# Choosing experts for the dense blocks first, with the low parts on VectorE and three of eight one-hot rows on ScalarE

## The chip, the core and the metric

The kernel runs on one core of a Trainium2 chip. The metric is the device time of one execution in microseconds. Before the change it was 3673.62 (median of three runs, 3673.24 to 3675.31).

## What is computed

One inference step of two layers for 512 prompt tokens and 32 sample tokens, model width 1024. Layer 0 mixes with sliding-window attention and a gated linear recurrence, layer 1 with a convolution module. After each mixer comes the same retrieval from 128 x 128 = 16384 experts of one neuron each, and only this retrieval is touched here:

```python
q = (xb @ w_q).reshape(blk, PEER_HEADS, 2, PEER_DKH)            # 8 heads, two halves
sc = jnp.einsum('nhpd,hpkd->nhpk', q, sub_keys)                 # scores against 128 keys
sv, si = lax.top_k(sc, 16)
cand = sv[:, :, 0, :, None] + sv[:, :, 1, None, :]              # 16 x 16 pairs
cidx = si[:, :, 0, :, None] * 128 + si[:, :, 1, None, :]
fv, fi = lax.top_k(cand, 16)
eidx = jnp.take_along_axis(cidx, fi, axis=-1)
gate = jax.nn.softmax(fv, axis=-1)
act = gelu(jnp.einsum('nd,nhed->nhe', xb, u_tab[eidx]))
y = jnp.einsum('nhe,nhed->nd', gate * act, v_tab[eidx])
```

## The kernel before, in words

Tokens come in five blocks: three dense blocks of 128 prompt tokens (n = 0, 1, 2), and two "lone" blocks, n = 3 (the last 128 prompt tokens) and n = 4 (the 32 samples; 4 x 32 rows, so it has 2 heads per partition in place of 8). The dense blocks compute all 16384 experts with matmuls and weigh them by a gate that is zero for experts not chosen. The lone blocks gather their experts' rows from DRAM one by one and work on VectorE.

Experts go in 128 tiles of 128, each with a unit tile (rows of u) and a value tile (rows of v), 256 tiles a layer. For fp32 accuracy each tile is split in two parts: ScalarE copies it to the high part (`hi`, line 1004, `ring<-raw`), and another engine subtracts this for the low part (`lo`); before the change that is GpSimd for a layer's first 48 tiles (line 1872) and VectorE for the rest (`low`, line 1551). TensorE then does 24 matmuls a unit tile (line 849) or 18 a value tile (line 861). ScalarE applies gelu to a unit's result (line 1075, `ga`). The first 48 tiles (AHEAD) are units; their results are written to DRAM (`units_ahead`) and come back later, since the gates aren't there yet. They pass through four ring slots and four raw buffers, and a unit's result through two PSUM banks: tile i+3's hi copy waits for unit i-1, its matmuls wait for the low part and for the gelu of two units before.

The choice (`select`, lines 1436 to 1523, VectorE) is cut in 15 parts: part 0 forms 50 candidate pairs a head, parts 1 to 4 take the best 16, parts 6 to 14 pick their numbers (`pick`, lines 1487, 1496, 1503). ScalarE takes the Exp of the gate (line 1063), which needs two table loads against gelu. For a dense block TensorE transposes what was chosen (`choice`, line 818), and ScalarE copies it to slT (line 1121): key 1, key 2 and gate of each of 128 rows, along the free dimension.

The gate matrix is made in groups of 8 tokens, 16 groups a block, 48 a layer. For each token VectorE makes two one-hot tiles of 128x128 in `onehots`: key 2 for all eight tokens in one comparison (line 1534), key 1 times the gate with one instruction a token (line 1539). TensorE multiplies them (`gate_group`, line 832), ScalarE copies the result to `stage` (lines 1107, 1113). After 8 groups SyncE writes the 4 MB of `stage` to DRAM (`gate_matrix`, line 433), and the next group's copy waits for this. Buffers for one-hots and for results hold two groups.

Order is written out by hand, a list for each engine, with semaphores between. `FRONT` is how many tiles are stepped through before the first group, `TILES_AFTER[g]` how many after group g; `TILES_BEFORE` is their running sum. The choices before the change stand in the order n = 4, 3, 0 ahead of the first group, then n = 1 and n = 2 beside the groups of blocks 0 and 1. A block's first group needs slT, which needs the whole choice before. After the groups SyncE waits for the gate matrix to be in DRAM, fetches the first gate tile (line 444) and stored unit (line 450), VectorE multiplies them (line 1562), ScalarE and VectorE split the product (lines 1083, 1569), and TensorE starts on value tiles. From there units and values alternate, and VectorE works through gathered rows (lines 1583, 1591) between low parts.

Of the kernel before, what the change touches and what calls it, by code (L numbers as in the profile page):

```python
# [28 lines left out]
P = 128  # L29
# [39 lines left out]
AHEAD, FRONT = 48, 24  # L69
# [36 lines left out]
TILES_AFTER = [0] * (ND // 8)  # L106
for _g in range(ND // 8):
    if _g < 32:
        TILES_AFTER[_g] = {1: 1, 3: 1, 5: 1, 7: 2}.get(_g % 8, 0)
TILES_AFTER[39] = 2  # L110
TILES_BEFORE = [FRONT + sum(TILES_AFTER[:_g]) for _g in range(ND // 8)]
EXP_BEFORE = {3: 0, 8: 1, 19: 2}
# [79 lines left out]
def build(nc, xT, stream, utab, vtab, params, consts, mconsts, reset, keysT, kcacheT, vcache, kvcache_n, state_h, convT,  # L192
          yT, kwin_p, vwin_p, hs_p, cb_p, kwin_s, vwin_s, hs_s, cb_s):
    ctx = ExitStack()
    with ctx:
# [84 lines left out]
        with ExitStack() as z:  # L280
# [27 lines left out]
            slT = sb("slT", [P, 2, 3, P], F32, z)  # L308
# [225 lines left out]
        s_oh = sem("key1_onehots_ready")  # L534
        s_oha = sem("key2_onehots_ready")
# [53 lines left out]
        def _(pe):  # L589
# [220 lines left out]
            def choice(l, n):  # L810

                pe.wait_ge(s_sel, NTILE * l + 3 + n)
# [182 lines left out]
        def _(act):  # L995
# [47 lines left out]

            def retrieval(l):
# [15 lines left out]
            def select_exp(l, i):  # L1060
                H = HEADS[(LONE + DENSE)[i]]
                act.wait_ge(s_gx, NTILE * l + i + 1)
                A.activation(sel[:, 2, 0:H, :], r16[:, 0:H, :], ACT.Exp).then_inc(s_ge, 1)

            def experts(l):
# [53 lines left out]
                for n in DENSE:  # L1119
                    act.wait_ge(s_selT, NDB * l + n + 1)  # L1120
                    A.activation(slT[:, n % 2, :, :], PB[0][:, 0, 0:3 * P].rearrange("p (i r) -> p i r", i=3),
                                 ACT.Copy).then_inc(s_slT, 1)
                    for q in range(16):
                        stage_group(n, q)
                        if q == 6 and n + 1 < NDB:
                            select_exp(l, 3 + n)
# [233 lines left out]
        def _(dve):  # L1360
# [75 lines left out]
            def select(l, i, part):  # L1436

                n = (LONE + DENSE)[i]
# [31 lines left out]
                elif part == 4:  # L1470
                    if done >= 1:
                        dve.wait_ge(s_ge, done)
                    if i >= 3:
                        dve.wait_ge(s_selT, NDB * l + i - 2)
                    elif i == 0 and l:
                        dve.wait_ge(s_selT, NDB * l)
# [48 lines left out]
            def onehots(l, n, q):  # L1525
# [6 lines left out]
                if n * 16 + q >= 2:  # L1532
# [3 lines left out]
                                ALU.is_equal).then_inc(s_oha, 1)  # L1536
                for j in range(8):
# [3 lines left out]
                    if j < 7:  # L1541
                        ch.done(m)
                ch.sync()
                m.then_inc(s_oh, 1)

            def experts(l):
# [57 lines left out]
                for i in range(AHEAD - 3, N_EXP):  # L1604
                    for j in range(ready_by(i - 1), ready_by(i)):
# [461 lines left out]
```

## Time and profile before

| | |
|---|---|
| profiled execution | 3672.08 us, its span 3670.3 us |
| mean granted TensorE clock | 0.947 |
| TensorE matmul busy | 3262.9 us (89%) |
| VectorE busy | 2843.0 us (77%) |
| ScalarE busy | 1284.1 us (35%) |
| GpSimd busy | 1461.5 us (40%) |
| DMA | 807.86 MB, mean 220 GB/s |

Busy shares are means over stages with different limits, so a stage is read by itself: first the busy time of each engine in it, then which wait ends last there. In a row of the timeline a start is followed by a duration; with a count, the duration runs from the first start to the last end. A duration has a short tail that the next instruction of the engine overlaps, so a repeated instruction's price is the distance of two starts. The two layers run the same program in their retrieval.

### The profile page before, as it was taken

The numbers are of one execution on the slowest core, as the hardware profiler recorded it, in microseconds if no ns is written. First come the engines' busy times: TensorE is split into PE (matmuls) and PEld (weight loads), VectorE is DVE, ScalarE is ACT, GpSimd is POOL, SyncE is SP. The second block draws the span as 40 slices with busy tenths as digits, with TensorE's granted clock in tenths as the row PEclk, the third lists the DMA queues.
The fourth block names the chain that finished last, engine by engine and source line by source line (L and its number), as shares of the span: only waits on it lengthen the run. The fifth ranks groups of instructions, "written<-read, shape, count | busy, mean of one in ns | idle before, by whom it ended". The sixth has DMA issues, their size and how long they took to land. (4 is left out here: it accounts for less than half of the span.)

```text
span 3670.3 us, 49481 instructions
## 1 busy us (share of the span) xinstructions
PE 3262.9 (89%) x18573; PEld 2976.5 (81%) x18573; DVE 2843.0 (77%) x5704; ACT 1284.1 (35%) x1735; POOL 1461.5 (40%) x856
## 2 busy tenths in 40 slices
PE   5876899978789999999987879997878999999998
PEld 5876789977778888888877648997767888888887
DVE  4425547999878888888866983799986888888887
ACT  3443222444433333333323222244444333333332
POOL 2210232733135555555542202273213555555553
PEclk9987699989899999999998989998899999999999
DMA  3110121534389999999971142153338999999997
GB/s 116 53 50 1 60 87 61 175 115 165 139 314 371 365 366 362 362 366 363 357 239 58 47 18 79 54 175 124 147 148 291 375 368 361 358 368 364 360 360 260
DMA packets 424991, 807.86 MB, mean 220 GB/s; under 512 B 233953, under 2 KB 259105, under 8 KB 421281
## 3 DMA queue, kind: packets, MB, share of 16 engines
q1 hardware_dynamic: 318960, 454.23, 36.6%
q0 software_dynamic: 94560, 344.45, 25.3%
q10 hardware_dynamic: 11232, 6.01, 1.3%
q8 instruction: 148, 2.42, 0.3%
q14 instruction: 91, 0.74, 0.1%
HBM read 729.52 MB, written 76.08 MB: 219 GB/s over the span
## 5 line engine op out<-in xcount | busy, mean ns | idle before, releaser
L849 PE MATMUL bank<-hh,ring 128*128 128x384 f32 x4096 | 1097.3, 341 | 18.4 <-POOL ring L1872 10.2
L1872 POOL TENSOR_TENSOR ring<-raw,ring 128x1024 fp32r<-128x1024 f32 x182 | 496.9, 2737 | 1110.2 <-ACT ring L1004 1107.3
L861 PE MATMUL bank<-ring,wh 128*128 128x512 f32 x3072 | 831.8, 393 | 22.1 <-DVE wl L1569 22.1
L849 PEld LDWEIGHTS bank<-hh,ring 128*128 128x128 f32 x4096 | 752.8, 191 | 27.9 <-POOL ring L1872 14.6
L1004 ACT ACTIVATE ring<-raw 128x1024 fp32r<-128x1024 f32 x598 | 622.5, 1054 | 241.4 <-PE bank L849 131.1
L849 PE MATMUL bank<-hl,ring 128*128 128x384 f32 x2048 | 692.3, 338 | 0.0
L861 PEld LDWEIGHTS bank<-ring,wh 128*128 128x128 f32 x3072 | 576.5, 188 | 134.5 <-DVE ring L1551 22.7
L1551 DVE TENSOR_TENSOR ring<-raw,ring 128x1024 fp32r<-128x1024 f32 x416 | 508.1, 1222 | 205.7 <-ACT ring L1004 205.5
L1903 POOL DMA_INDIRECT rows<-in_utab,gidx x320 | 450.4, 1408 | 481.8 <-DVE av L1583 378.9
L1903 POOL DMA_INDIRECT rows<-in_vtab,gidx x320 | 490.9, 1534 | 368.6 <-DVE acc L1591 316.1
L610 PE MATMUL bank<-hh,ring 128*128 128x272 f32 x2752 | 494.8, 299 | 78.7 <-DVE hl L1377 43.8
L610 PEld LDWEIGHTS bank<-hh,ring 128*128 128x128 f32 x2752 | 409.8, 196 | 92.7 <-issue 51.5
L861 PE MATMUL bank<-ring,wl 128*128 128x512 f32 x1536 | 474.2, 390 | 0.0
L1075 ACT ACTIVATE ga<-bank 128x384 f32<-128x384 f32 x256 | 124.5, 486 | 990.5 <-PE bank L849 990.3
L1591 DVE SCALAR_TENSOR_TENSOR acc<-rows,wv,acc 128x1024 f32<-128x1024 f32 x316 | 404.3, 1279 | 12.3 <-DVE acc L1591 0.5
L849 PEld LDWEIGHTS bank<-hl,ring 128*128 128x128 f32 x2048 | 390.6, 191 | 6.1
L1583 DVE CUSTOM_DVE_ANT_0 rows<-rows,htok 128x1024 f32<-128x1024 f32 x320 | 381.6, 1218 | 1.0 <-DMA rows<-in_utab,gidx 1.0
L861 PEld LDWEIGHTS bank<-ring,wl 128*128 128x128 f32 x1536 | 289.3, 188 | 64.4
L832 PE MATMUL bank<-oh 128*128 128x128 f32 x1536 | 220.6, 305 | 120.2 <-DVE oh L1539 111.6
L832 PEld LDWEIGHTS bank<-oh 128*128 128x128 f32 x1536 | 207.6, 216 | 132.8 <-DVE oh L1539 123.9
L610 PE MATMUL bank<-hl,ring 128*128 128x272 f32 x1376 | 293.5, 295 | 0.0
L1539 DVE TENSOR_SCALAR oh<-con,slT 128x128 f32<-128x128 f32 x768 | 256.7, 403 | 0.0
(297 smaller groups left out, 3101.5 us busy)
## 6 DMA issues: line engine op xcount, KB each, us to landing
raw<-in_stream SPq DMA_DIRECT2D x342, 512.0 KB, 4.9
raw<-in_vtab SPq DMA_DIRECT2D x256, 512.0 KB, 7.9
gate_matrix<-stage SPq DMA_DIRECT2D x24, 2048.0 KB, 9.3
gt<-gate_matrix SPq DMA_DIRECT2D x256, 192.0 KB, 9.6
units_ahead<-ga SPq DMA_DIRECT2D x96, 192.0 KB, 2.9
gv<-units_ahead SPq DMA_DIRECT2D x96, 192.0 KB, 8.3
rows<-in_utab,gidx POOLq DMA_INDIRECT x320, 8.2
rows<-in_vtab,gidx POOLq DMA_INDIRECT x320, 7.9
```

The source lines that it names most:

```text
L610: m = T.matmul(PA[t % 2][:, a, 0:HALF], w[:, ring_slot(t), k * P:(k + 1) * P], h[:, k, a * HALF:(a + 1) * HALF], start=(k == 0 and i == 0) ...
L832: m = T.matmul(PA[e % 2][:, i // 4, (i % 4) * P:(i % 4 + 1) * P], oh2[:, e % 2, i, :], oh1[:, e % 2, i, :], start=True, stop=True)
L849: m = T.matmul(PB[1][:, (e + 1) % 2, 0:ND], w[:, ring_slot(t), k * P:(k + 1) * P], h[:, k, 0:ND], start=(k == 0 and i == 0), stop=(k == KC ...
L861: m = T.matmul(psum[c][:, a, :], w[:, v_n % WSLOT, c * P:(c + 1) * P], v[:, ring_slot(t), 512 * a:512 * a + 512], start=(v_n == 0 and i == ...
L1004: A.activation(ring_hi[:, ring_slot(t), :], raw[b][:], ACT.Copy).then_inc(s_hi, 1)
L1075: A.activation(ga[:, e % ASLOT, :], PB[1][:, (e + 1) % 2, 0:ND], ACT.Gelu).then_inc(s_ga, 1)
L1539: m = V.tensor_scalar(oh1[:, e % 2, j, :], iota, slT[:, n % 2, 0, c:c + 1], slT[:, n % 2, 2, c:c + 1], ALU.is_equal, ALU.mult)
L1551: V.tensor_tensor(ring_lo[:, ring_slot(t), :], raw[raw_buffer(t)][:], ring_hi[:, ring_slot(t), :].bitcast(F32), ALU.subtract).then_inc(s_l ...
L1583: V.tensor_tensor_reduce(out=rows[:, slot, :], in0=rows[:, slot, :], in1=htok[b][:, :], scale=1.0, scalar=0.0, op0=ALU.mult, op1=ALU.add, ...
L1591: V.scalar_tensor_tensor(out=acc[b][:, :], in0=rows[:, slot, :], scalar=wv[b][:, j:j + 1], in1=acc[b][:, :], op0=ALU.mult, op1=ALU.add).th ...
L1872: nc.gpsimd.tensor_tensor(ring_lo[:, slot, :], raw[buf][:], ring_hi[:, slot, :].bitcast(F32), ALU.subtract).then_inc(s_lo, 1)
L1903: nc.gpsimd.indirect_dma_start(out=rows[:, g % ROW_SLOTS, :], out_offset=None, in_=vtab if is_v else utab, in_offset=bass.IndirectOffsetOn ...
```

## The change

The order of choices becomes 0, 1, 2, then 4, 3 (`SEL_ORDER`). Ahead of the first group VectorE makes only the choice of block 0, in nine quanta with a tile step after each; the lone blocks' choices stand beside the groups of block 2, two parts a group. `FRONT` is 12, and `TILES_AFTER` goes on with its pattern in the third block: 31 tiles inside the groups, so that units 43 to 47 follow the last group. The low parts of tiles 3 to 47 go from GpSimd to VectorE (`ahead` is gone from GpSimd's program). Key 1's rows 0 to 2 of each group (`ACT_OH`) go to ScalarE: Abs(key - iota) and then Relu(gate - gate x distance), which is the gate where the distance is 0, and 0 elsewhere; gates are positive and distances whole. For it slT gets a fourth row, the negated gate.

```diff
-AHEAD, FRONT = 48, 24
+AHEAD, FRONT = 48, 12
...
+TILES_AFTER = [{1: 1, 3: 1, 5: 1, 7: 2}.get(_g % 8, 0) for _g in range(ND // 8)]
+TILES_AFTER[3] = TILES_AFTER[19] = TILES_AFTER[35] = 2
+TILES_AFTER[47] = 0
...
+SEL_ORDER = DENSE + LONE
+SEL_QUANTA = [(0,), (1, 2), (3, 4, 5), (6, 7), (8,), (9, 10), (11,), (12, 13), (14,)]
+EXP_BEFORE = {3: 0}
+ACT_OH = 3
...
+            def onehots(l, n, q):
+
+                e = (ND // 8) * l + n * 16 + q
+                if n * 16 + q >= 2:
+                    act.wait_ge(s_gm, e - 1)
+                if e:
+                    act.wait_ge(s_oha, e)
+                for j in range(ACT_OH):
+                    c = 8 * q + j
+                    ch.done(A.activation(dist[:, j, :], iota, ACT.Abs, scale=-1.0,
+                                         bias=slT[:, n % 2, 0, c:c + 1]))
+                ch.sync()
+                for j in range(ACT_OH):
+                    c = 8 * q + j
+                    m = A.activation(oh1[:, e % 2, j, :], dist[:, j, :], ACT.Relu,
+                                     scale=slT[:, n % 2, 3, c:c + 1], bias=slT[:, n % 2, 2, c:c + 1])
+                m.then_inc(s_oha, 1)
...
                 for n in DENSE:
                     act.wait_ge(s_selT, NDB * l + n + 1)
-                    A.activation(slT[:, n % 2, :, :], PB[0][:, 0, 0:3 * P].rearrange("p (i r) -> p i r", i=3),
-                                 ACT.Copy).then_inc(s_slT, 1)
+                    ch.done(A.activation(slT[:, n % 2, 0:3, :], PB[0][:, 0, 0:3 * P].rearrange("p (i r) -> p i r", i=3),
+                                         ACT.Copy))
+                    ch.sync()
+                    A.activation(slT[:, n % 2, 3, :], PB[0][:, 0, 2 * P:3 * P], ACT.Copy, scale=-1.0)\
+                        .then_inc(s_slT, 1)
+                    act.wait_ge(s_slT, NDB * l + n + 1)
+                    onehots(l, n, 0)
                     for q in range(16):
+                        if q + 1 < 16:
+                            onehots(l, n, q + 1)
                         stage_group(n, q)
...
-                for j in range(8):
+                for j in range(ACT_OH, 8):
...
-                for i in range(3):
-                    for part in range(NPART):
-                        select(l, i, part)
+                dve.wait_ge(s_lo, t0 + 3)
+                for i in range(FRONT):
+                    if i < len(SEL_QUANTA):
+                        for part in SEL_QUANTA[i]:
+                            select(l, 0, part)
+                    tile_step(i)
                 for n in DENSE:
                     for q in range(16):
+                        g = 16 * n + q
                         onehots(l, n, q)
                         if n + 1 < NDB and q >= 1:
-                            select(l, 3 + n, q - 1)
-                dve.wait_ge(s_lo, t0 + AHEAD)
+                            select(l, n + 1, q - 1)
+                        if n + 1 == NDB and q >= 1:
+                            for part in (2 * q - 2, 2 * q - 1):
+                                select(l, NDB + part // NPART, part % NPART)
+                        if g:
+                            for m in range(TILES_AFTER[g - 1]):
+                                tile_step(TILES_BEFORE[g - 1] + m)
```

VectorE, the end of the choice that the first group waits for and the first groups. `pick` and `eidx` belong to the choice, `small` is the signal that it is complete, `ring<-raw,ring` is a low part, `oh` a one-hot tile. Before:

```order
L1509 TENSOR_TENSOR sel<-sel,r 128x128
L1512 TENSOR_SCALAR sel<-eidx 128x128
L1514 TENSOR_SCALAR sel<-sel 128x128
L1516 SCALAR_TENSOR_TENSOR sel<-sel,eidx 128x128
L1523 MEMSET small 128x1
L1534 TENSOR_TENSOR oh<-con,slT 128x1024
L1539 TENSOR_SCALAR oh<-con,slT 128x128 x8
L1534 TENSOR_TENSOR oh<-con,slT 128x1024
L1539 TENSOR_SCALAR oh<-con,slT 128x128 x8
L1445 CAST sif<-si 128x256
```

After, the same place, with the low parts of tiles 11 to 14 between the choice and the first group:

```order
L1536 TENSOR_TENSOR sel<-sel,r 128x128
L1539 TENSOR_SCALAR sel<-eidx 128x128
L1541 TENSOR_SCALAR sel<-sel 128x128
L1543 SCALAR_TENSOR_TENSOR sel<-sel,eidx 128x128
L1550 MEMSET small 128x1
L1575 TENSOR_TENSOR ring<-raw,ring 128x1024 x4
L1561 TENSOR_TENSOR oh<-con,slT 128x1024
L1566 TENSOR_SCALAR oh<-con,slT 128x128 x5
L1561 TENSOR_TENSOR oh<-con,slT 128x1024
L1566 TENSOR_SCALAR oh<-con,slT 128x128 x5
L1474 CAST sif<-si 128x256
```

Five rows a group are left on VectorE, and low parts stand among choice and one-hots.

ScalarE, from the copy of slT (first row) through the first groups; `stage` is the copy of a group's result, `ring<-raw` a hi copy, `ga` a gelu. Before:

```order
L1121 ACTIVATE slT<-bank 128x384
L1107 ACTIVATE stage<-bank 128x8x64 x2
L1113 ACTIVATE stage<-bank 128x8x128
L1004 ACTIVATE ring<-raw 128x1024
L1075 ACTIVATE ga<-bank 128x384
L1113 ACTIVATE stage<-bank 128x8x128 x2
```

After, with `dist` the distances and `oh<-dist,slT` the finished rows:

```order
L1141 ACTIVATE slT<-bank 128x384
L1144 ACTIVATE slT<-bank 128x128
L1055 ACTIVATE dist<-con,slT 128x128 x3
L1060 ACTIVATE oh<-dist,slT 128x128 x3
L1055 ACTIVATE dist<-con,slT 128x128 x3
L1060 ACTIVATE oh<-dist,slT 128x128 x3
L1127 ACTIVATE stage<-bank 128x8x64 x2
L1055 ACTIVATE dist<-con,slT 128x128 x3
L1060 ACTIVATE oh<-dist,slT 128x128 x3
L1133 ACTIVATE stage<-bank 128x8x128
L1006 ACTIVATE ring<-raw 128x1024
L1095 ACTIVATE ga<-bank 128x384
```

A group's rows stand one group ahead of its stage copy, and each tile step's hi copy and gelu stand behind them.

SyncE's queue, from the layer's last gate write (first row) to the first gate tile asked for (`gt`). Before:

```order
L433 DMA gate_matrix<-stage 128x4096 x2
L444 DMA gt<-gate_matrix 128x6x64
L450 DMA gv<-units_ahead 128x384
L438 DMA units_ahead<-ga 128x384
L428 DMA raw<-in_stream 128x1024
```

After:

```order
L435 DMA gate_matrix<-stage 128x4096 x2
L440 DMA units_ahead<-ga 128x384
L428 DMA raw<-in_vtab 128x1024
L440 DMA units_ahead<-ga 128x384
L430 DMA raw<-in_stream 128x1024
L440 DMA units_ahead<-ga 128x384
L428 DMA raw<-in_vtab 128x1024
L446 DMA gt<-gate_matrix 128x6x64
L452 DMA gv<-units_ahead 128x384
```

Three unit writes and three loads now stand between the write and the first gate tile.

## Rows read from the trace of the kernel before

**Rows 1.** Stages of layer 0: length, busy PE, PEld, DVE, ACT, POOL, PEclk, DMA, GB/s.
```profile
750.00:852.00 102.00, 82.42 (x508) 80.77 (x508) 96.67 (x245) 47.61 (x43) 30.36 (x10) 0.91 0.31 111
852.00:957.00 105.00, 82.58 (x497) 80.61 (x496) 97.77 (x245) 46.85 (x41) 32.27 (x10) 0.89 0.41 152
...
1100.00:1600.00 500.00, 500.00 (x2460) 445.44 (x2459) 427.32 (x597) 170.11 (x244) 268.45 (x187) 1.00 1.03 366
```
**Rows 2.** Waits between 750 and 1024: total us, times, longest.
```profile
POOL ring L1872 <- ACT ring L1004: 183.8, 18, 31.2
...
PE bank L832 <- DVE oh L1539: 53.4, 26, 5.5
```
**Rows 3.** ScalarE's slT copies: start, duration; in brackets idle before, its releaser.
```profile
749.97 0.49 ACT L1121 ACTIVATE slT<-bank 128x384 f32<-128x384 f32 x1 [10.45 <-PE bank L818]
...
957.40 0.49 ACT L1121 ACTIVATE slT<-bank 128x384 f32<-128x384 f32 x1
```
**Rows 4.** TensorE, timeline of layer 0; the last two from layer 1's chain.
```profile
1020.37 2.05 PE L832 MATMUL bank<-oh 128*128 128x128 f32 x16 [1.13 <-DVE oh L1539]
...
1050.45 2.04 PE L861 MATMUL bank<-ring,wh 128*128 128x512 f32 x4 [11.38 <-DVE wl L1569]
...
2802.05 6.35 PE bank L861 x18
...
2820.86 8.21 PE bank L861 x36
```
**Rows 5.** VectorE, undisturbed groups of block 2 in layer 0, timeline.
```profile
967.60 2.13 DVE L1539 TENSOR_SCALAR oh<-con,slT 128x128 f32<-128x128 f32 x8
969.65 1.22 DVE L1534 TENSOR_TENSOR oh<-con,slT 128x1024 f32<-128x1024 f32 x1
```
**Rows 6.** VectorE, choices in layer 0, timeline.
```profile
645.39 2.37 DVE L1445 CAST sif<-si 128x64 f32<-128x64 uint32 x1
...
661.13 0.29 DVE L1445 CAST sif<-si 128x256 f32<-128x256 uint32 x1
...
662.75 2.40 DVE L1456 TENSOR_TENSOR cand<-sv 128x16 f32<-128x16 f32 x1
...
673.62 2.66 DVE L1487 TENSOR_TENSOR pick<-pos,con 128x2400 f32<-128x2400 f32 x1
676.32 4.73 DVE L1496 TENSOR_TENSOR pick<-pick,cidx 128x2400 f32<-128x2400 f32 x1
```
**Rows 7.** A low part on GpSimd beside them, two on VectorE, timeline.
```profile
675.16 3.38 POOL L1872 TENSOR_TENSOR ring<-raw,ring 128x1024 fp32r<-128x1024 f32 x1 [1.67 <-ACT ring L1004]
...
1059.63 2.35 DVE L1551 TENSOR_TENSOR ring<-raw,ring 128x1024 fp32r<-128x1024 f32 x2
```
**Rows 8.** VectorE's groups by shape, 540 to 1050: busy us, mean ns, idle before.
```profile
L1539 DVE TENSOR_SCALAR oh<-con,slT 128x128 f32<-128x128 f32 x384 | 125.0, 395 | 0.0
L1534 DVE TENSOR_TENSOR oh<-con,slT 128x1024 f32<-128x1024 f32 x48 | 69.9, 1456 | 21.4 <-ACT slT L1121 14.0 <-PE bank L832 7.3
```
**Rows 9.** ScalarE, hi copies of two tile steps in a row, timeline.
```profile
665.70 1.06 ACT L1004 ACTIVATE ring<-raw 128x1024 fp32r<-128x1024 f32 x1 [2.72 <-PE bank L849]
...
669.86 1.06 ACT L1004 ACTIVATE ring<-raw 128x1024 fp32r<-128x1024 f32 x1 [2.73 <-PE bank L849]
```
**Rows 10.** ScalarE: one pointer operand (timeline), none (by line), stage copies (timeline).
```profile
2007.83 9.75 ACT L1324 ACTIVATE diag<-con,par 128x128 f32<-128x128 f32 x33
...
L1041 ACT ACTIVATE zq<-bank 128x128 f32<-128x128 f32 x16 | 4.2, 262 | 0.0
...
1007.41 3.81 ACT L1113 ACTIVATE stage<-bank 128x1024 f32<-128x1024 f32 x2 [1.96 <-PE bank L832]
```
**Rows 11.** The gate matrix's way: SyncE's issues and ScalarE's wait, timeline.
```profile
989.88 0.80 SPq L433 DMA_DIRECT2D gate_matrix<-stage  x2
...
1002.64 1.04 ACT L1107 ACTIVATE stage<-bank 128x512 f32<-128x512 f32 x1 [3.61 <-DMA gate_matrix<-stage]
...
1038.27 0.37 SPq L444 DMA_DIRECT2D gt<-gate_matrix  x1
```

More of the change, by code:

```diff
@@ L307, in build @@
             sel = sb("sel", [P, 3, 8, 16], F32, z)
-            slT = sb("slT", [P, 2, 3, P], F32, z)
+            slT = sb("slT", [P, 2, 4, P], F32, z)
+            dist = sb("dist", [P, ACT_OH, P], F32, z)
         with ExitStack() as z:
@@ L1436, in select @@
             def select(l, i, part):
-                n = (LONE + DENSE)[i]
+                n = SEL_ORDER[i]
                 H = HEADS[n]
@@ L1472, in select @@
                         dve.wait_ge(s_ge, done)
[L1473 to L1476, printed above, removed]
+                    if i >= 1:
+                        dve.wait_ge(s_selT, NDB * l + min(i, NDB))
                     V.tensor_tensor(r16[:, 0:H, :], fv[:, 0:H, :], fv[:, 0:H, 0:1].to_broadcast([P, H, 16]),
@@ L1592, in row, with tile_step @@
                                                in1=acc[b][:, :], op0=ALU.mult, op1=ALU.add).then_inc(s_rd, 1)
-                for i in range(3):
-                    for part in range(NPART):
-                        select(l, i, part)
+                def tile_step(i):
+                    for j in range(ready_by(i - 1) if i else 3, ready_by(i)):
+                        low(t0 + j)
+                dve.wait_ge(s_lo, t0 + 3)
[4 more added lines that the diff above has]
+                    tile_step(i)
                 for n in DENSE:
                     for q in range(16):
+                        g = 16 * n + q
                         onehots(l, n, q)
                         if n + 1 < NDB and q >= 1:
-                            select(l, 3 + n, q - 1)
-                dve.wait_ge(s_lo, t0 + AHEAD)
+                            select(l, n + 1, q - 1)
[5 more added lines that the diff above has]
+                                tile_step(TILES_BEFORE[g - 1] + m)
                 n_row = 0
-                for i in range(AHEAD - 3, N_EXP):
-                    for j in range(ready_by(i - 1), ready_by(i)):
-                        low(t0 + j)
+                for i in range(TILES_BEFORE[-1], N_EXP):
+                    tile_step(i)
                     if i >= AHEAD - 1 and tile_at(i + 1)[1]:
@@ L1878, in lo_run @@
                     lo(t, ring_slot(t), raw_buffer(t))
-            def ahead(l):
-                def tile_step(i):
-                    for j in range(ready_by(i - 1) if i else 3, min(AHEAD, ready_by(i))):
-                        lo(T_EXP[l] + j, ring_slot(T_EXP[l] + j), raw_buffer(T_EXP[l] + j))
-                for i in range(FRONT):
-                    tile_step(i)
-                for g in range(ND // 8):
-                    for m in range(TILES_AFTER[g]):
-                        tile_step(TILES_BEFORE[g] + m)
             def gather_rows(l):
```

25 lines of the change are left out of this document (8 added, 17 removed).

## The prediction, made before the changed kernel had run

> **What bounds the kernel now.** I read the table of stages first [rows 1]. From 1100 to 1600 us TensorE is busy for 500 of 500 us: the long stream over values and units can't be shortened by this change, it can only start sooner. What the change touches is the stretch before it, from the first unit tile (about 638) to the first value tile at 1050.45 in layer 0, and the same again in layer 1, 1751.6 later (first value tile at 2802.05) [rows 4]. There TensorE has gaps (82 of 102, 83 of 105 us), while VectorE is busy for 97 of 102 and 98 of 105. The waits say who is waited for: ScalarE stood 10.45 us in front of the first slT copy, which waits for the first choice [rows 3], TensorE 53.4 us for one-hots (line 1539) [rows 2] and 11.4 us for the first gated value tile [rows 4]. So VectorE sets the pace in front of and inside the gate groups, and after them the round trip of the gate matrix through DRAM does.
>
> Four dates fix the stretch [rows 3, 4]: slT copied at 749.97 for block 0 and at 957.40 for block 2 (two blocks of groups in 207.4), last gate group done on TensorE at 1022.42, first value matmul at 1050.45. I price the change against these, for one layer, and double it.
>
> **VectorE's own work.** Undisturbed, a group's eight rows take 2.05 from first start to the next instruction's (0.256 each, with a tail of 0.08), the wide comparison 1.22 less the same tail, 1.14 [rows 5]. With five rows left it is 1.14 + 5 x 0.256 = 2.42. One 8-head choice: six picks over 2400 elements at 2.65 and three over two thirds of that at 1.8 make 21.3 [rows 6]; from its first cast at 661.13 to its first pick at 673.62 it is 12.5, of which an addition of 16 elements that took 2.40 is over 2 of stretch, so about 10; its end I put at 1.7 with the synchronising: 33 us. The 2-head choice ran 15.7 (645.39 to 661.13) with some 4 of stretch (its cast of 64 elements took 2.37, one of 256 took 0.29): 11.5. A low part is 1.22, one start every 1.15 [rows 7].
>
> **The stretch by GpSimd.** A pass over 2400 elements took 2.66 and the next one 4.73, from 676.32, while GpSimd worked on a low part from 675.16 to 678.54; in layer 0 the mean of line 1539 is 395 ns against 0.256 + 0.08 us, that of line 1534 1456 against 1220 [rows 5 to 8]. That is 384 x 0.059 + 48 x 0.236 = 34 us, and if half of the choices' long passes are stretched by up to 2 us, as the one shown, and a few small operations too, about 55 a layer. After the change GpSimd has nothing to do before the gathers, so I count all VectorE work at its undisturbed price. The Trainium skill (GPSIMD Engine Reference, section 1, Specifications) says that GpSimd shares its SBUF interfaces with VectorE and contends with two-port modes and two-input operations; the sum would keep its place by that rule. By a reading of the trace in which the stretch has another source it is rival 3's second price.
>
> **Front, term a.** VectorE goes straight into the dense choice at 645.39 (end of key search). It has 33 us of choice and, before the choice's last quantum, 8 low parts at 1.15: ready at about 688. TensorE must do 11 units first; the hi copies, each released by a unit's end, come every 4.16 [rows 9]; a unit (number 5) ended at 665.7, so unit 10 ends at 686.5 or, with two low parts some 2 us late, near 692. Three transposes 0.9, slT copy 0.49 and the added negated copy of 0.3 behind a semaphore: slT at 693 instead of 750, **-57**. Half of the 24 units that stood here move: they are in terms b and c. Over the whole stretch VectorE gets 45 low parts (52 us) and loses three rows in each of 48 groups (37 us); the two lone choices (44.5) go from before the first group to the third block.
>
> **Groups, term b.** ScalarE gets per group three Abs and three Relu of 128x128. Line 1324 does the like (one pointer operand) in 9.75 us for 33, 0.295 each, so 0.39 with the tail; without a pointer a 128x128 copy is 0.26 [rows 10]. So a second pointer is about 0.13, the Relu 0.43 a start, and a group 3 x 0.295 + 0.15 (semaphore and tail) + 3 x 0.43 = **2.3 us**. No row shows a Relu with two pointers: below, 0.295 gives 1.9; above, nothing overlapped (0.39 and 0.53 each, two semaphores) gives 3.0. I take 2.3, since the 33 in a row do overlap.
> Per block of 16 groups (blocks 0 and 1, 11 tiles in each):
> - VectorE 16 x 2.42 + 33 + 11 x 1.15 = 84
> - ScalarE 16 x 2.3 + 16 x 1.83 (stage copies, two in 3.81 [rows 10]) + 11 x 1.4 (a tile step: 4.16 less the 2.73 idle [rows 9]) + 2.9 (Exp with its table loads, an estimate) + 0.9 = 85
> - TensorE 16 x 2.05 + 11 x 4.16 + 0.9 = 79
>
> Three engines within 6 us of each other, in fixed orders, with two one-hot buffers: no one of them runs without waits. ScalarE's order decides: one-hots of q+1, stage copy of q (waits for TensorE), hi copy (waits for a unit), gelu. Laying out a block by hand: its 85 us, plus 5 where the first stage copy of the second half waits for the gate write (the copy of 1002.64 waited for the write issued at 989.88: 13 us after the previous copy [rows 11], 8 of them filled), plus 5 at the block's end (unit 4.16 and transposes between the last stage copy and slT), plus 4 where two units follow each other behind one group: 99. It was 102 to 105. The second block has the gate write late at its start too: 101. In the third VectorE has 39 + 44.5 + 11 x 1.15 = 96, 5 of it behind the last group, and waits some 10 for hi copies: 101. Every hand-over costs about 0.12 (the 0.08 of tail and as an estimate half of that for the semaphore), one and a half a group: 8. The granted clock in blocks 0 and 1 was 0.91 and 0.89 of 2.4 GHz [rows 1], a mean of both levels; a block's 79 us of TensorE's work then become 88, of which I put a quarter on the path: 6 for three blocks. Sum 99 + 101 + 101 + 8 + 6 = 315 against 1022.42 - 749.97 = 272.5: **+42.5**.
>
> **Tail, term c.** Before: four units, then TensorE waits 11.4; gate tile asked for at 1038.27, matmul at 1050.45 [rows 4, 11]: 28.0 from the last group. Now seven units (43 to 49) stand there, 7 x 4.16 = 29.1 us; by the same rows the gated tile would be ready at 2 (stage copy) + 13 + 12.2 = 27, and SyncE, which passes two unit writes and two loads before it asks, is there by about 11. Hidden: **+1.1**. The first value tile after the wait took 6.35 us instead of half of 8.21 [rows 4]: gone, **-2.5**. The gathers wait for the lone choices, now 5 us after the last one-hots, and for the last stage copy; they are no later than before.
>
> Per layer -57 + 42.5 + 1.1 - 2.5 = -15.9, both layers -32. The profiled execution took 3672.1 (span 3670.3 and 1.8 around it), 1.5 under the median: 3640, against 3673.6.
>
> **Rivals.**
> 1. VectorE alone sets the pace, ScalarE's work is hidden. Its sum from 645.39 is 143 + 48 x 2.42 + 48 x 1.15 = 314; last one-hots at 954, two block ends of 6 and a group: 968; plus 29 is 997, -56 a layer, 3560. For it: VectorE was 95% busy before (97 of 102 [rows 1]). Against: ScalarE's 85 of 99, and its place in front of every low part.
> 2. Slower, ScalarE's rows as price: at 3.0 us a group it is 0.7 x 48 = 34 more a layer, as ScalarE is on the path in nearly every group: +18, 3707. It decides from 16/48 = 0.33 us over my 2.3. For it: the Relu's second pointer was never timed here, and the pass from Abs to Relu needs a wait. Against: the 33 diagonals in a row. The Trainium skill (ScalarE: Activation LUTs, Rules for kernel authors) gives relu to VectorE, not ScalarE; here 0.73 against 0.256 a row agrees that it is dearer, and only the balance of the engines can pay it. Its price there (section What ACT_TABLE_LOAD costs) of 93 ns a pointer would make the group an estimated 2.2.
> 3. No difference: VectorE's 33 low parts inside the groups wait for hi copies that stand late in ScalarE's order. GpSimd waited 183.8 us for them and no one minded [rows 2]; now one-hots queue behind. Half a microsecond more for each eats the 16: 3672. Or the stretch doesn't go: 55 more of VectorE work makes the last one-hots come near 1010, and the time 3675.
>
> **How the numbers follow.** Forecast 0.58, with its own range 3615 to 3665 (the second pointer from 0.295 up, the hand-laid waits a third less or more). Rival 1 0.12, rival 2 0.14, rival 3 0.16. 0.2% is 7 us, about what these runs tell apart. Faster: the forecast but for 0.02, rival 1, and a little of rival 3: 0.73. Same 0.13, slower 0.14. The range 3592 to 3690 leaves out most of rival 1 and the worse half of rival 2.
>
> **What would show it.** First slT at 693 (within 5); line 1539's successor at 334 without a tail; blocks of 99 to 105 between slT dates; ScalarE 85% or more busy between them and named first among TensorE's and VectorE's waits; the first value tile at about 1034, with no wait over 3 us in front of it. Wrong if a group's six ScalarE rows take over 2.6, if VectorE is 95% busy in the blocks, or if the stream's 500 of 500 is broken.

## The result, and the profile after

The changed kernel took 3609.8 us (median of four runs, 3605.8 to 3614.5) against 3674.5 for the kernel before on the same chip (3673.2 to 3677.0): a ratio of 0.9824, interval 0.9807 to 0.9841. The forecast of 3640 had the direction right. The gain is 64.7 us instead of 33.6: the time lies 5 us beyond the forecast's own range of 3615 to 3665, and inside the wide one of 3592 to 3690. The profiled execution has a span of 3606.0, against 3670.3.

The table of stages after, with the columns of [rows 1]. The stretches are those between the copies of slT; the last is the long stream.

```profile
687.00:784.00 97.00, 81.61 (x523) 79.54 (x522) 82.23 (x208) 81.99 (x141) 0.00 (x0) 0.95 0.41 149
784.00:883.00 99.00, 82.37 (x530) 80.32 (x529) 82.50 (x208) 83.14 (x144) 0.00 (x0) 0.95 0.46 168
883.00:990.00 107.00, 83.62 (x496) 81.72 (x495) 92.29 (x251) 81.60 (x140) 0.00 (x0) 0.87 0.39 141
...
1100.00:1600.00 500.00, 500.00 (x2462) 445.85 (x2461) 430.52 (x588) 168.67 (x242) 269.05 (x187) 1.00 1.03 365
```

VectorE falls from 97 of 102 to 82 of 97, ScalarE rises from 47 to 82, GpSimd is empty, and the stream is as full as before. TensorE, VectorE and ScalarE are within 2 us of each other in the first two blocks, so busy time alone names none of them as the bound.

ScalarE's timeline, answering to [rows 3]: the three slT copies of layer 0, and behind the first copy the rows of a group and the start of the next.

```profile
687.12 0.48 ACT L1141 ACTIVATE slT<-bank 128x384 f32<-128x384 f32 x1
...
687.95 0.99 ACT L1055 ACTIVATE dist<-con,slT 128x128 f32<-128x128 f32 x3
688.97 1.26 ACT L1060 ACTIVATE oh<-dist,slT 128x128 f32<-128x128 f32 x3
690.26 0.98 ACT L1055 ACTIVATE dist<-con,slT 128x128 f32<-128x128 f32 x3
...
784.43 0.48 ACT L1141 ACTIVATE slT<-bank 128x384 f32<-128x384 f32 x1
...
882.68 0.48 ACT L1141 ACTIVATE slT<-bank 128x384 f32<-128x384 f32 x1
```

The blocks are 97.3 and 98.3 long, and a group's six rows take 690.26 - 687.95 = 2.31.

TensorE's timeline at the layer's last group and first value tile, answering to [rows 4]:

```profile
985.12 3.65 PE L834 MATMUL bank<-oh 128*128 128x128 f32 x16 [5.02 <-DVE oh L1566]
...
1021.14 1.16 PE L863 MATMUL bank<-ring,wh 128*128 128x512 f32 x4 [1.22 <-DVE wl L1593]
```

The last group ends at 988.77 (before: 1022.42), the first value matmul starts at 1021.14 (1050.45), after a wait of 1.22 instead of 11.38.

VectorE and ScalarE by line and shape, 540 to 1050, columns as in [rows 8]:

```profile
L1566 DVE TENSOR_SCALAR oh<-con,slT 128x128 f32<-128x128 f32 x240 | 65.6, 341 | 0.0
L1060 ACT ACTIVATE oh<-dist,slT 128x128 f32<-128x128 f32 x144 | 60.7, 484 | 1.6
L1561 DVE TENSOR_TENSOR oh<-con,slT 128x1024 f32<-128x1024 f32 x48 | 58.4, 1218 | 10.4 <-ACT slT L1144 10.4
L1055 ACT ACTIVATE dist<-con,slT 128x128 f32<-128x128 f32 x144 | 46.4, 390 | 0.3
L1523 DVE TENSOR_TENSOR pick<-pick,cidx 128x2400 f32<-128x2400 f32 x8 | 21.2, 2654 | 0.1
```

VectorE's stretch, the extra time of its operations beside GpSimd's low parts, is gone: a row is 341 ns (395 before), the comparison 1218 (1456), and all eight passes are at 2.65 [rows 6 had one of 4.73]. The Relu with two pointers is 0.09 over the Abs with one.

Waits from 687 to 990, columns as in [rows 2]:

```profile
PE bank L834 <- DVE oh L1566: 47.7, 20, 5.0
DVE ring L1575 <- ACT ring L1006: 34.0, 16, 5.4
ACT stage L1133 <- PE bank L834: 24.5, 15, 6.7
ACT stage L1127 <- DMA gate_matrix<-stage: 11.8, 5, 3.1
...
PE bank L834 <- ACT oh L1060: 4.6, 1, 4.6
```

These are to be read as one chain: TensorE waits for VectorE's one-hots, VectorE stands before them with a low part that waits for ScalarE's hi copy, and that copy stands in ScalarE's order behind six rows and a stage copy that waits for TensorE.

And the gate matrix's way at the layer's end, answering to [rows 11] (SyncE, then ScalarE and VectorE):

```profile
990.85 0.80 SPq L435 DMA_DIRECT2D gate_matrix<-stage  x2
...
1004.73 0.37 SPq L446 DMA_DIRECT2D gt<-gate_matrix  x1
1005.14 4.00 SPq L452 DMA_DIRECT2D gv<-units_ahead  x1
```

```profile
1006.45 0.49 ACT L1095 ACTIVATE ga<-bank 128x384 f32<-128x384 f32 x1 [4.01 <-DMA units_ahead<-ga]
...
1016.54 0.56 DVE L1586 TENSOR_TENSOR gv<-gv,gt 128x384 f32<-128x384 f32 x1 [5.28 <-DMA gv<-units_ahead]
```

SyncE asks for the gate tile 13.9 us after the write. The stored unit is multiplied 11.4 us after SyncE begins to ask for it (1005.14 to 1016.54); before it was 7.2 (1038.68 to 1045.86). TensorE's units behind the last group take a little more than their 29.1, since one gelu waits 4.01 for its buffer and TensorE 1.65 for this gelu, and then it waits the 1.22.

### The profile page after: what moved, and what is told of

The parts are those of the page before. It is cut to its first block, busy times and chain, and to the rows that moved or that the text cites. A ratio compares the mean times of both kernels' runs of the same rounds, so it can differ in the third digit from the quotient of the medians.

```text
span 3606.0 us, 49776 instructions
## 1 busy us (share of the span) xinstructions
PE 3253.4 (90%) x18573; PEld 2970.3 (82%) x18573; DVE 2745.2 (76%) x5506; ACT 1486.4 (41%) x2317; POOL 1185.2 (33%) x766
## 4 chain that ended last, share of the span: by engine, by line
PE 69%; DVE 17%; DMA 5%; ACT 4%; issue 3%; POOL 1%; SPq 0%; DVEq 0%; ACTq 0%; POOLq 0%
PE bank L863 29%; PE bank L851 20%; PE bank L612 12%; DVE cv L1879 5%; DMA gate_matrix<-stage 3%; PE bank L834 2%; DVE ring L1575 2%; DVE oh L1566 1%; PE bank L746 1%; DVE oh L1561 1%; DVE pick L1523 1%; PE bank L762 1%; DVE pick L1514 1%; DVE eidx L1530 1%; PE bank L600 1%
## 5 line engine op out<-in xcount | busy, mean ns | idle before, releaser
L1575 DVE TENSOR_TENSOR ring<-raw,ring 128x1024 fp32r<-128x1024 f32 x506 | 617.5, 1222 | 279.0 <-ACT ring L1006 278.5
L851 PEld LDWEIGHTS bank<-hh,ring 128*128 128x128 f32 x4096 | 756.4, 191 | 32.4 <-POOL ring L1908 9.6
L1006 ACT ACTIVATE ring<-raw 128x1024 fp32r<-128x1024 f32 x598 | 622.8, 1054 | 214.2 <-DMA raw<-in_stream 97.3
L1908 POOL TENSOR_TENSOR ring<-raw,ring 128x1024 fp32r<-128x1024 f32 x92 | 223.3, 2436 | 675.7 <-ACT ring L1006 673.0
L851 PEld LDWEIGHTS bank<-hl,ring 128*128 128x128 f32 x2048 | 392.6, 192 | 6.1
L612 PEld LDWEIGHTS bank<-hl,ring 128*128 128x128 f32 x1376 | 226.1, 196 | 0.0
```

The costliest lines, as they stand in the source:

```text
L612: m = T.matmul(PA[t % 2][:, a, 0:HALF], w[:, ring_slot(t), k * P:(k + 1) * P], h[:, k, a * HALF:(a + 1) * HALF], start=(k == 0 and i == 0) ...
L851: m = T.matmul(PB[1][:, (e + 1) % 2, 0:ND], w[:, ring_slot(t), k * P:(k + 1) * P], h[:, k, 0:ND], start=(k == 0 and i == 0), stop=(k == KC ...
L1006: A.activation(ring_hi[:, ring_slot(t), :], raw[b][:], ACT.Copy).then_inc(s_hi, 1)
L1575: V.tensor_tensor(ring_lo[:, ring_slot(t), :], raw[raw_buffer(t)][:], ring_hi[:, ring_slot(t), :].bitcast(F32), ALU.subtract).then_inc(s_l ...
L1908: nc.gpsimd.tensor_tensor(ring_lo[:, slot, :], raw[buf][:], ring_hi[:, slot, :].bitcast(F32), ALU.subtract).then_inc(s_lo, 1)
```

## The experiments

All are built from the changed kernel and timed in three rounds beside the kernel before, whose median was 3674.2 to 3675.2 in every set. "Changed" is the 3609.8 above. The first three undo one part each, the fourth two of the three. Nothing was edited ahead of the retrieval, and still its first copy stands anywhere from 629.5 to 636.2 us in the profiled executions; so dates are counted from that copy, and a difference of a few us between two times is not told apart.

**All rows back on VectorE.**

```diff
-ACT_OH = 3
+ACT_OH = 0
...
-                    onehots(l, n, 0)
                     for q in range(16):
-                        if q + 1 < 16:
-                            onehots(l, n, q + 1)
                         stage_group(n, q)
```

> The changed kernel (3609.8 us), but with all eight rows of a group on VectorE; ScalarE makes none. VectorE gets 48 x 3 x 0.256 = 37 us a layer more, ScalarE loses 48 x 2.35 = 113. Theory A (each engine's work lies partly on the path, because the three are level and run in fixed orders): VectorE alone sets the pace, blocks of 84 + 12 and about 6 at the end, 101 to 104 for 97 and 98 and the third near 115; 12 to 20 us a layer, 3635 to 3650. Theory B (VectorE sets the pace already in the changed kernel, ScalarE is hidden): the whole 37 a layer, 3684. Theory C (rows on ScalarE bring nothing, the gain is from the order and the low parts): 3610.

3624.0 (3620.9 to 3626.7), ratio 0.9864 (0.9848 to 0.9881): 14 slower than changed, under the 3635 to 3650 of the first reading and over the 3610 of the third. VectorE is now the bound, as the stages from 700 show (columns as above):

```profile
700.00:780.00 80.00, 64.17 (x421) 62.55 (x419) 79.89 (x210) 41.54 (x36) 0.00 (x0) 0.96 0.37 134
800.00:880.00 80.00, 66.11 (x421) 64.67 (x419) 78.87 (x206) 41.26 (x36) 0.00 (x0) 0.94 0.37 132
```

VectorE is busy for 79.9 and 78.9 of 80, and the blocks are 98.8 and 102.5 long: 1.5 and 4.3 more than changed. 144 rows at 0.256 are 37 us of VectorE work a layer; with ScalarE's share of that work gone only 7 are seen. With the two other parts in place, the three rows on ScalarE are worth 14 us of the 65.

**Low parts back on GpSimd.**

```diff
                     for j in range(ready_by(i - 1) if i else 3, ready_by(i)):
+                        if j < AHEAD:
+                            continue
                         low(t0 + j)
...
+            ahead(0)
             gather_rows(0)
```

> The changed kernel, but with the low parts of tiles 3 to 47 on GpSimd again. VectorE loses 45 x 1.15 = 52 us of work a layer. Theory A (GpSimd's low parts stretch what VectorE does beside them, up to 2 us each time): 55 us of stretch come back, so no gain: 3600 to 3630, with VectorE's single rows of 2 us and more in the trace again. Theory B (the stretch was of another source): VectorE is 52 us a layer lighter, with ScalarE and TensorE next in line: some 20 a layer faster, 3570.

3613.4 (3607.0 to 3615.1), ratio 0.9828 (0.9812 to 0.9844): not to be told from changed. By line and shape, 540 to 1050:

```profile
L1911 POOL TENSOR_TENSOR ring<-raw,ring 128x1024 fp32r<-128x1024 f32 x56 | 154.8, 2768 | 307.7 <-ACT ring L1006 307.3
L1566 DVE TENSOR_SCALAR oh<-con,slT 128x128 f32<-128x128 f32 x240 | 105.1, 502 | 0.0
L1561 DVE TENSOR_TENSOR oh<-con,slT 128x1024 f32<-128x1024 f32 x48 | 69.5, 1447 | 29.6 <-PE bank L834 15.7 <-ACT slT L1144 13.9
L1523 DVE TENSOR_TENSOR pick<-pick,cidx 128x2400 f32<-128x2400 f32 x8 | 25.4, 3169 | 0.1
...
L1530 DVE TENSOR_REDUCE eidx<-pick 128x48 f32<-128x2400 f32 x8 | 21.1, 2643 | 0.1
```

The stretch comes back with GpSimd's work and by nothing else: rows 341 to 502 in the mean, the comparison 1218 to 1447, one of the three kinds of long pass 2654 to 3169. The means hide how it comes. Most rows are as short as ever and a few take over 2 us:

```profile
L1566 DVE TENSOR_SCALAR oh<-con,slT x240: 328/335/2550, 699.0 to 990.2; 128x128 f32<-128x128 f32 x120
```

(x240: shortest, median, longest in ns.) Between 640 and 1025 us, 32 of VectorE's operations take over 0.3 us more than others of their kind, each at most 2.3 more, and every one of them overlaps a subtraction on GpSimd; in the changed kernel there is none. Their excess is 64 us in sum, 55 of it in the three groups above (39.5 + 11.0 + 4.2). The same sum in the kernel before is 60, so the prediction's estimate of 55 was sound. The low parts that leave VectorE are 45 x 1.15 = 52. So with ScalarE's rows in place the move exchanged one for the other and the time hardly changed. With all rows on VectorE it is otherwise, as the fourth experiment shows.

**The old order of choices** and of tiles, the two other parts kept (the tiles of each group and the semaphore counts that follow are left out here).

```diff
-AHEAD, FRONT = 48, 12
+AHEAD, FRONT = 48, 24
...
-SEL_ORDER = DENSE + LONE
+SEL_ORDER = LONE + DENSE
...
-                    if i < len(SEL_QUANTA):
-                        for part in SEL_QUANTA[i]:
-                            select(l, 0, part)
+                    for part in (2 * i, 2 * i + 1):
+                        if part < 3 * NPART:
+                            select(l, part // NPART, part % NPART)
```

> The changed kernel, but with the old order of choices and of tiles: lone blocks 4 and 3 and then block 0 ahead of the first group, 24 tiles in front, 22 inside the groups, four units after the last. Low parts on VectorE and three rows on ScalarE stay. Theory A: the first slT is at 116 us after the layer's lone tokens as before the change (77 us of choice plus 23 low parts at 1.15 and their waits), 61 later; blocks 0 and 1 as now, 97 each; the third without the lone choices near 60 instead of 106; tail 28 instead of 32: 10 to 15 us a layer slower, 3630 to 3640. Theory B (the early first choice is what pays, the gates' third block costs nothing extra): 50 a layer or more slower, 3710.

3658.4 (3655.5 to 3664.1), ratio 0.9957 (0.994 to 0.9974): both readings missed, 18 above the one's 3640 and 52 under the other's 3710. Its slT dates say why. The first block's slT comes as late as before (118.2 us after the retrieval's start; before 118.3, changed 57.3), since three choices and 23 low parts stand in front of it. Blocks 0 and 1 take 98.2 and 98.8 (before 101.8 and 105.6), but the third, which has no choice in it, 72.7 instead of 65.0. Its stage, here and then in the kernel before, and a wait here:

```profile
946.00:1019.00 73.00, 53.48 (x325) 50.39 (x324) 44.39 (x100) 64.84 (x121) 0.00 (x0) 0.84 0.35 134
```

```profile
957.00:1022.00 65.00, 46.38 (x322) 43.99 (x322) 56.21 (x145) 32.73 (x24) 4.99 (x2) 0.95 0.37 142
```

```profile
PE bank L836 <- ACT oh L1062: 11.3, 4, 5.5
```

VectorE is busy for 44 us instead of 56, ScalarE for 65 of 73 instead of 33 of 65, and TensorE waits 11.3 for ScalarE's rows: without a choice beside them ScalarE's rows stand in the way. The granted clock is lower too, 0.84 instead of 0.95; no run separates its part.

**The order alone**: all rows on VectorE and the low parts on GpSimd, that is both edits of the first two experiments together.

> The new order of choices with its tile steps, but all eight rows on VectorE and the low parts of tiles 3 to 47 on GpSimd. Theory A (the three parts of the change act one by one): rows back cost 14, low parts back 3 to 4, by the two runs that undid them singly, so 3620 to 3630; the order alone brings about 48 of the 65. Theory B (the parts cover for each other: VectorE, with its rows and GpSimd's stretch, is the bound again as soon as both are back): per layer 48 groups of 3.9, choices 66 + 44 and 25 of stretch are over 320 between the first slT and the last one-hots, and the time is 3645 to 3660.

3667.2 (3661.7 to 3669.6), ratio 0.9976 (0.9965 to 0.9988). Parts that acted one by one would have given 3628 (14 and 4 over changed); even the second reading (3645 to 3660) was too low. Stages from 700:

```profile
700.00:780.00 80.00, 65.11 (x403) 63.38 (x403) 79.97 (x206) 38.90 (x34) 26.75 (x8) 0.90 0.35 125
800.00:880.00 80.00, 64.98 (x398) 63.42 (x397) 79.69 (x208) 37.24 (x34) 27.84 (x9) 0.91 0.45 164
```

VectorE is busy for all of both. The first slT stands at 61.8, 56.5 sooner than before, and the blocks, which now hold the lone choices too, take 106.9, 106.0 and 110.0: 50.4 of it is given back. From the first slT to the last one-hots VectorE is busy for 304 of 319 us here, 288 of 303 with the low parts on it (first experiment), 265 of 295 with the rows on ScalarE (second), 253 of 298 with both (changed).

The five versions as a table (us under the kernel before):

| order | rows on ScalarE | low parts on VectorE | gain |
|---|---|---|---|
| new | no | no | 7 |
| old | yes | yes | 16 |
| new | no | yes | 50 |
| new | yes | no | 61 |
| new | yes | yes | 65 |

(The kernel before is the old order without the other two.) So what a part is worth depends on the others: low parts on VectorE bring 4 us beside ScalarE's rows, which is within the noise, and 43 without them, where VectorE is busy throughout and the 15 us a layer that it is spared are felt. The new order moves work from a place where TensorE waits anyway into the blocks. It pays only if VectorE has room there, and either relief makes most of that room. With the old order both reliefs together bring 16; one of them alone was not run there.

**Four units in place of seven behind the last group.**

```diff
+TILES_AFTER[40] = TILES_AFTER[42] = TILES_AFTER[44] = 1
```

> The changed kernel, but with three more tiles inside the third block's groups, so that 2 + 2 units instead of 5 + 2 follow the last group. Theory A (after the last group the way of the gate matrix through DRAM takes 28 us, whatever stands beside it, and the third block is set by VectorE): tail 28 instead of 32, third block up to 4 longer: 3602 to 3612. Theory B (the units were needed as cover): 3 x 4.16 = 12.5 us of waiting a layer more, 3635.

3610.5 (3606.6 to 3615.7), ratio 0.9824 (0.9806 to 0.9842): no difference. The last group ends 3.6 us later in layer 0, counted from the first slT, and TensorE waits again:

```profile
PE bank L864 <- DVE wl L1594: 11.5, 1, 11.5
```

From the last group to the first value matmul it is 28.1 us (before 28.0, changed 32.4). So four units leave the gate matrix's way through DRAM bare, and with seven the way itself is longer: the stored unit is multiplied 7.2 us after it is asked for here, 11.4 in changed. What the shorter tail gives, the third block (108.9 against 106.1) and a stream of 853.8 against 851.2 take back. What makes the stored unit late beside more unit writes and loads was not tried.

**Three more Abs a group on ScalarE**, written where the real ones overwrite them.

```diff
+                for j in range(ACT_OH):
+                    c = 8 * q + j
+                    ch.done(A.activation(oh1[:, e % 2, j, :], iota, ACT.Abs, scale=-1.0,
+                                         bias=slT[:, n % 2, 0, c:c + 1]))
```

> The changed kernel with three more Abs a group on ScalarE, whose results the Relus overwrite: 48 x 0.88 = 42 us a layer more for ScalarE, nothing for the others. Theory A: ScalarE is on the path about half of the time: 20 to 40 us a layer, 3650 to 3690. Theory B (VectorE sets the pace, ScalarE is hidden): under 8 us a layer, 3610 to 3625.

3654.9 (3652.7 to 3658.8), ratio 0.9945 (0.9928 to 0.9962): 45 slower, for 288 x 0.295 = 85 us of added work. Half of what is added to ScalarE is seen. The waits from 690 to 1020 show how:

```profile
PE bank L834 <- DVE oh L1570: 49.9, 20, 5.9
DVE ring L1579 <- ACT ring L1006: 49.4, 21, 6.8
...
PE bank L851 <- ACT ga L1099: 12.6, 5, 4.6
```

TensorE's wait for VectorE is nearly as in changed (47.7), VectorE's for the hi copy has grown from 34.0 to 49.4, and TensorE's own wait for ScalarE's gelu from 1.4 to 12.6. ScalarE is felt through VectorE and directly. VectorE as the only bound is refuted.

**Two rows a group on ScalarE** in place of three (`ACT_OH = 2`).

> The changed kernel with two of eight rows on ScalarE instead of three: ScalarE 48 x 0.7 = 33 us a layer less, VectorE 12 us more. Theory A (ScalarE on the path half of the time): 0 to 10 a layer faster, 3590 to 3610. Theory B (VectorE alone): 12 a layer slower, 3634.

3606.0 (3604.9 to 3607.9), ratio 0.9816 (0.9799 to 0.9832): 4 under changed, with intervals that overlap. 35 us less a layer on ScalarE (48 x 0.725) and 12 more on VectorE come out about even.

The other five go after the chain of waits itself.

**Hi copy first**: ScalarE makes a group's first tile step before the next group's rows and the stage copy.

```diff
+                        ta, tb = TILES_AFTER[16 * n + q], TILES_BEFORE[16 * n + q]
+                        if ta:
+                            tile_step(tb)
                         if q + 1 < 16:
                             onehots(l, n, q + 1)
                         stage_group(n, q)
...
-                        for m in range(TILES_AFTER[16 * n + q]):
-                            tile_step(TILES_BEFORE[16 * n + q] + m)
+                        for m in range(1, ta):
+                            tile_step(tb + m)
```

> The changed kernel with ScalarE's order inside a group altered: the first tile step's hi copy and gelu stand ahead of the next group's rows and the stage copy, not behind. No work is added or taken away. VectorE waited 43 us in layer 0 for hi copies between 633 and 1010. Theory A (the wait of low parts for hi copies is on the path): half of it goes, 8 to 15 a layer faster, 3580 to 3595. Theory B (these waits are filled anyway): 3605 to 3612.

3594.0 (3591.2 to 3603.1), ratio 0.9779 (0.9762 to 0.9795): 16 under changed, as the first reading has it at its upper end.

**Low part one group later** on VectorE, ScalarE as in changed.

```diff
-                        if g:
-                            for m in range(TILES_AFTER[g - 1]):
-                                tile_step(TILES_BEFORE[g - 1] + m)
+                        if g > 1:
+                            for m in range(TILES_AFTER[g - 2]):
+                                tile_step(TILES_BEFORE[g - 2] + m)
+                for m in range(TILES_AFTER[46]):
+                    tile_step(TILES_BEFORE[46] + m)
```

> The changed kernel with VectorE's low parts one group later in its order (after the one-hots of the group two behind), ScalarE's order as it is. Theory A: VectorE's wait for hi copies shrinks from 43 us to under 10, of which half was on the path: 8 to 15 a layer faster, 3580 to 3595. Theory B (it waits elsewhere instead, or TensorE then waits for the low parts): 3605 to 3615.

3599.2 (3596.3 to 3601.8), ratio 0.9794 (0.9777 to 0.9811): 11 under changed, with no run in common, though the intervals of the ratios just meet; it falls between the two readings. Waits from 687 to 985 of the hi-copy-first kernel:

```profile
PE bank L834 <- DVE oh L1569: 30.4, 16, 5.9
DVE ring L1578 <- ACT ring L1006: 22.8, 9, 4.8
PE bank L834 <- ACT oh L1060: 16.7, 5, 5.4
```

and of the kernel with the later low parts:

```profile
DVE oh L1561 <- PE bank L834: 23.4, 7, 6.7
PE bank L834 <- ACT oh L1060: 14.3, 4, 4.6
PE bank L834 <- DVE oh L1566: 11.8, 10, 4.1
```

Both take away part of the same chain: TensorE's wait for VectorE's one-hots falls from 47.7 to 30.4 and 11.8, and VectorE's for hi copies from 34.0 to 22.8 and 4.8. And both turn a part of it into a new wait, TensorE's for ScalarE's rows (16.7 and 14.3; changed 4.6).

**Hi copy first, and two rows.**

> The high copy ahead of the next group's rows on ScalarE, and two rows a group there in place of three. Theory A (ScalarE is still the engine most on the path, so its work counts once more): 3586 to 3591, 3 to 8 under the copy-first run. Theory B (with the high copy first, VectorE sets the pace, and a row back costs 48 x 0.256 x 2 = 25, a third of it seen): 3598 to 3604.

3594.2 (3591.1 to 3597.2), ratio 0.9783 (0.9766 to 0.9799): nothing over hi copy first in the median. It falls between the two readings, and neither is borne out.

**Hi copy first, and low part later.**

> The high copy ahead of the next group's rows on ScalarE, and the low part one group later on VectorE. Theory A (both take away the same wait, VectorE's for a high copy): 3588 to 3596, little over the copy-first run's gain of 16. Theory B (two different waits: TensorE's for the unit and VectorE's for the copy): the gains of 16 and 11 add up, 3580 to 3586.

3594.6 (3591.2 to 3599.2), ratio 0.978 (0.9763 to 0.9796): no better than hi copy first alone, so the gains don't add. Waits from 687 to 990:

```profile
PE bank L834 <- ACT oh L1060: 18.1, 3, 7.9
...
PE bank L834 <- DVE oh L1569: 9.1, 8, 4.8
DVE ring L1578 <- ACT ring L1006: 6.2, 5, 2.7
```

The two waits of the chain are small, as with the later low parts alone, and TensorE's wait for ScalarE's rows has taken their place: both edits had taken the same wait.

**All three.**

> High copy first, low part one group later, two rows on ScalarE. Theory A (same wait): 3584 to 3593. Theory B (gains add): 3576 to 3583. If VectorE is the bound by then, two rows are worse than three and this is 3 to 8 slower than the version with three.

3583.5 (3579.5 to 3586.3), ratio 0.9749 (0.9733 to 0.9765): the best version, 91 under the kernel before and 26 under changed, just under the lower edge of the first reading. The warning of the third, that two rows would now be worse than three, is refuted. Waits from 687 to 990:

```profile
ACT stage L1127 <- DMA gate_matrix<-stage: 38.7, 10, 5.6
...
PE bank L834 <- ACT oh L1060: 25.6, 5, 7.9
...
PE bank L834 <- DVE oh L1569: 18.7, 14, 5.0
...
DVE ring L1578 <- ACT ring L1006: 8.6, 4, 2.9
```

With VectorE's wait for hi copies nearly gone (8.6), much of what is left is ScalarE's: it waits for the gate write (38.7, from 11.8), and TensorE for its rows (25.6). A row less brings 11 us against the version before it, where it brought 4 without the other edits and nothing with the first of them. But those two are within the noise: by the profiled executions, one each and with both layers' retrievals alone counted, a row less takes off 7, 6 and 10 us. So it is shown that it helps in the last version, and not that it helps there only. Whether the gate write's wait is the next bound was not tried.

## Why the prediction was right, and where its size was off

Dates are counted from the retrieval's first copy on ScalarE, 631.7 before and 629.8 after.

- **Term a, the front: -57, measured -61.0** (slT of block 0; in layer 1 also -61.0). Expected 693, came at 687.12: nearer to the sooner of the two dates that the prediction worked out for unit 10, and 1.9 of the difference is that the whole retrieval starts sooner. But the order is worth this only with room in the blocks; alone it brings 7 us in all.
- **Term b, the groups: +42.5, measured +29.2 in layer 0 and +24.1 in layer 1.** This is the term that was mis-sized. The blocks laid out by hand were 99 + 101 + 101 = 301; measured 97.3 + 98.3 + 106.1 = 301.7. The 8 for hand-overs and 6 for the lower clock, put on top, did not appear. The granted clock was 0.95 in the first two blocks, not 0.91 and 0.89 as before, so for these the reason of the 6 fell away; whether the hand-overs were already in the laid-out waits can't be told, since the agreement is a sum of two blocks that were some 2 shorter and one that was 5 longer than laid out. In that third block VectorE is busy for 92 of 107 with both lone choices, the clock is 0.87, and TensorE waits 5.02 before the very last group.
- **ScalarE's six rows: 2.3, measured 2.31.** The Relu is 0.43 a start (0.48 with its tail), as bounded from the 33 diagonals. Rival 2 needed 2.63.
- **The stretch: about 55 a layer; 60 in the kernel before, 64 with the low parts back on GpSimd, none in changed.** What the prediction didn't say is that its end little more than pays for the 52 of low parts that VectorE gets.
- **Term c, the tail: +1.1, measured +4.3 (32.4 against 28.0), in layer 1 +6.5.** From the gate write to the first gate tile asked for it was 13.9, predicted as 13. But the stored unit came 11.4 after it was asked for instead of 7.2, so the gated tile was ready 32 after the last group and not at 27; the seven units lost 1.65 to a gelu that waits for its buffer's write, and 1.22 was waited for the gated tile. With four units behind the last group it is 28.1 and the time the same.
- **Term d, first value tiles at full clock: -2.5, measured -2.3** in layer 0 (stream of 851.2 against 853.4) and -1.2 in layer 1. With four units behind the last group, where TensorE waits 11.50 again, the stream is 853.8.

Per layer this is -29.7 and -31.6 where -15.9 was forecast. That the forecast had the direction rests on term a and on the blocks as laid out; that the sum of the blocks agrees to 1 us is in part luck, since two errors cancel. Another 3.0 us lie outside the retrieval (1.9 before it and 1.1 between the layers); no run assigns them to the change, and executions of one kernel differ by as much.

**The rivals.** VectorE alone (3560): refuted, since added ScalarE work is half seen, but near it lies something true: VectorE is busy for all of the stages from 700 when all rows and GpSimd's stretch are on it, and nearly so with the rows alone. ScalarE's price (3707): the mechanism is real, by the same run, and its condition didn't occur. Waits for hi copies (3672): they are there, 34.0 us in layer 0, and on the path: to relieve them brings 16 or 11. The half microsecond for each low part, beyond the forecast's blocks, that the rival needed did not come: the blocks' sum is as laid out. Its second price, that the stretch stays (3675), is refuted by the rows of 341 ns. Of the signs named beforehand, the rows at an undisturbed price (340 in the median, 348 at most) and the full stream held. The first slT was 5.9 from its 693, just beyond the 5 allowed (4.0 with the retrieval's own start taken out). The first two blocks were 1 to 2 shorter than the 99 named and the third 1 longer than the 105. ScalarE was busy for 84% in the first two and 76% in the third instead of 85% or more. The first value tile came at 1021.14 and not about 1034, with a wait of 1.22 in front of it. And TensorE's first wait is VectorE's, not ScalarE's, which stands behind it: the forecast named the right engines, and not the way in which one is felt through the other.

## What to carry to other kernels

Work moved from a stretch where the main engine waits anyway into one with three busy engines is worth what room the slowest of these has: count that engine's busy time there first, and price the edits together, since here the order's 7 us and the two reliefs' 16 made 65 together. When three engines in fixed orders share the pace, look for the operation that others queue behind (here the hi copy) and put it first; a wait that reads as one engine's is often another's, one step further back. Be wary of adding hand-overs on top of a block laid out by hand: here 14 us put on top so did not appear.

## What the runs showed of the hardware

- VectorE's stretch beside GpSimd's 128x1024 subtraction is not a general slowing: single operations take up to 2.3 us longer, about one such subtraction, and the others nothing. With the low parts on GpSimd it fell on 19 of 240 rows of 128x128 with a pointer operand, 7 of 48 comparisons of 1024 columns, 2 of 16 passes over 2400 elements with two tensors, and on single short ones, even an addition of 16 elements (0.17 to 2.40 us). It didn't fall on a reduction over 2400 elements (8 at 2643 ns in the mean, 4 of them beside such a subtraction), nor on the key search's MAX8 and FIND_INDEX8 there. GpSimd's own operation takes 2768 ns in the mean in that kernel against 2387 in the changed one, where all of them stand before the choices.
- On ScalarE a Relu of 128x128 with two pointer operands takes 94 ns more than an Abs with one (484 against 390 ns; no run parts the function from the operand), and of three in a row each overlaps the one before by about 0.09 us.
